# A decoder layer on one Trainium2 core: in the MLP's seven-product groups, two of the four weight sums are made by a GpSimd transfer that adds in SBUF, instead of by VectorE

## What is computed

```python
    merged = g[:, :, 0] * o_conv + g[:, :, 1] * o_fox + g[:, :, 2] * o_mem
    x = x + merged @ w_out
    h2 = _rms(x, norm2_g)
    x = x + jnp.square(jax.nn.relu(h2 @ w_up)) @ w_down
```

## Time and profile before

| | us |
|---|---|
| median of 3 runs (lowest, highest) | 1628.13 (1627.29, 1629.13) |
| the profiled execution | 1628.6 |
| its span in the profile | 1626.9 |
| busy: PE, DVE, ACT, POOL | 1616.9, 1169.6, 871.4, 4.8 |
| moved by DMA | 315.88 MB |

### The profile page before, as it was taken

One profiled execution on the slowest core, in us unless ns is written; L12 is line 12 of the kernel. 1 busy time (PEld: TensorE's weight loads), 2 busy tenths in 40 slices (PEclk: granted clock), 3 DMA queues, 4 the chain that ended last, 5 costly groups with the idle time before them and its releaser, 6 DMA issues.

```text
span 1626.9 us, 19902 instructions
## 1 busy us (share of the span) xinstructions
PE 1616.9 (99%) x7374; PEld 1339.8 (82%) x7374; DVE 1169.6 (72%) x1279; ACT 871.4 (54%) x1023; POOL 4.8 (0%) x13
## 2 busy tenths in 40 slices
PE   8999999999999999999999999999999999999998
PEld 7888888888888888888888888888888888888887
DVE  5856676555477777766765678887888788887777
ACT  5845445444455555544344566655665466556663
POOL 0000000000000000000000000000000000000000
PEclk9999999999999999999999999999999999999999
DMA  8856555555655666675565665566565655565554
GB/s 315 295 170 190 171 170 154 169 164 170 174 170 190 193 191 200 206 269 186 180 195 191 205 196 182 182 208 196 193 200 189 203 185 192 201 203 193 191 189 150
DMA packets 151780, 315.88 MB, mean 194 GB/s; under 512 B 9104, under 2 KB 9488, under 8 KB 150928
## 3 DMA queue, kind: packets, MB, share of 16 engines
q1 hardware_dynamic: 151696, 314.72, 61.0%
HBM read 312.59 MB, written 2.10 MB: 193 GB/s over the span
## 4 chain that ended last, share of the span: by engine, by line
PE 98%; DMA 1%; DVE 0%; ACT 0%; SPq 0%; issue 0%; DVEq 0%; ACTq 0%
PE bank L1954 42%; PE bank L1780 40%; PE bank L2057 9%; PE bank L1975 3%; PE bank L1799 2%; PE bank L1812 1%; DMA raw<-in_w_mem_kv 1%; PE bank L1907 0%; PE bank L1837 0%; PE bank L1868 0%; DVE wlo L1117 0%; PE bank L1927 0%; ACT whi L643 0%; PE bank L1832 0%; PE bank L1929 0%; DVE wide L1202 0%
## 5 line engine op out<-in xcount | busy, mean ns | idle before, releaser
L1117 DVE TENSOR_TENSOR wlo<-raw,whi 128x1024 fp32r<-128x1024 f32 x490 | 593.9, 1223 | 358.0 <-ACT whi L643 353.9
L643 ACT ACTIVATE whi<-raw 128x1024 fp32r<-128x1024 f32 x490 | 515.1, 1058 | 544.7 <-PE bank L1780 283.2
L1780 PE MATMUL bank<-whi,lhs_a 128*128 128x512 f32 x1280 | 400.5, 394 | 0.0
L1954 PE MATMUL bank<-whi,lhs_a 128*128 128x512 f32 x1248 | 385.0, 390 | 0.0
L1780 PEld LDWEIGHTS bank<-whi,lhs_a 128*128 128x128 f32 x1280 | 236.9, 188 | 46.8
L1954 PEld LDWEIGHTS bank<-whi,lhs_a 128*128 128x128 f32 x1248 | 233.7, 188 | 48.1
L1780 PE MATMUL bank<-wlo,lhs_a 128*128 128x512 f32 x640 | 249.8, 390 | 0.0
L1954 PE MATMUL bank<-wlo,lhs_a 128*128 128x512 f32 x624 | 242.9, 389 | 0.0
L1954 PE MATMUL bank<-whi,lhs_b 128*128 128x512 f32 x768 | 237.5, 390 | 0.0
L1954 PEld LDWEIGHTS bank<-whi,lhs_b 128*128 128x128 f32 x768 | 143.4, 188 | 29.4
L1780 PE MATMUL bank<-whi,lhs_b 128*128 128x512 f32 x512 | 158.1, 390 | 3.9 <-DVE wlo L1140 2.2
(11 more groups left out here) (241 smaller groups left out, 1503.5 us busy)
## 6 DMA issues: line engine op xcount, KB each, us to landing
raw<-in_w_in SPq DMA_DIRECT2D x208, 512.0 KB, 3.7
raw<-in_w_up SPq DMA_DIRECT2D x96, 512.0 KB, 4.0
raw<-in_w_down SPq DMA_DIRECT2D x96, 512.0 KB, 4.5
raw<-in_w_out SPq DMA_DIRECT2D x32, 512.0 KB, 3.7
raw_f<-in_w_up SPq DMA_DIRECT2D x16, 1024.0 KB, 5.0
raw_f<-in_w_down SPq DMA_DIRECT2D x16, 1024.0 KB, 5.0
raw<-in_w_mem_kv SPq DMA_DIRECT2D x30, 512.0 KB, 6.7
raw<-in_w_conv_out SPq DMA_DIRECT2D x16, 512.0 KB, 4.4
```

The source lines that it names most:

```text
L643: act.activation(whi[n % RING], raw[slot], ACT.Copy).then_inc(hi_ready, 1)
L1117: dve.tensor_tensor(wlo[n % RING], raw[plain(n) % RING], whi[n % RING].bitcast(F32), ALU.subtract).then_inc(lo_ready, 1)
L1780: last = pe.matmul(dst, lhs[:, part, k + kk, s], w[:, kk, :], start=(k + kk == 0 and i == 0), stop=(k + kk == tiles - 1 and i == 2))
L1954: last = pe.matmul(bank[2 * side + tok], lhs[:, part, PK * k + kk, P * tok:P * (tok + 1)], w[:, kk, :], start=(at + kk == 0 and i == 0), s ...
```

## The change

The weight sums are now made with plus signs, and the signs that this takes away move to the small sums of the activations (`s_sums`) and to the last step of `combine`. T1 and T3 are B11 + B12 and B22 + B12. They are made so:

- SP issues, ahead of each `raw_f` load, one more load of 512 KB that puts B12 twice (a repeated source) into `t_raw[:, 0:2]`. It waits for the same `lo_ready`, and also for `t_lo_ready` of the group before.
- GpSimd waits for this load (`t_begun`) and for `raw_f` (`fast_landed`), and issues a transfer from `raw_f[:, 1:3]` to `t_raw[:, 0:2]` in SBUF that adds. It signals `t_summed`.
- DVE's operation at line 1520 falls away. `t_sums` waits for `t_summed` and makes T2 and T4.
- ACT's first half of `t_hi` waits for `t_summed`, the second for T4.
- SP's loop over three quarters is written out.

```diff
             def load_ff(n, src):
                 if is_fast(n):
+                    q, blk, at, _ = ff_place(n)
                     if freed_by(n) < 0:
                         sp.wait_ge(merged_ready, NBD)
                     else:
-                        sp.wait_ge(lo_ready, base + (freed_by(n) + 1))
+                        sp.wait_ge(lo_ready, freed_by(n) + 1)
+                        sp.wait_ge(t_lo_ready, fast_index(q, blk, at))
+                    sp.dma_start(t_raw[:, 0:2, :], src[:, 0:1, 0:COLS].to_broadcast([P, 2, COLS])).then_inc(t_begun, 16)
                     sp.dma_start(raw_f[:].rearrange("p (k s) n -> p k (s n)", k=PK), src).then_inc(fast_landed, 16)
                     return
...
+            for f in range(FASTS * QUARTERS):
+                pool.wait_ge(t_begun, 16 * (f + 1))
+                pool.wait_ge(fast_landed, 16 * (f + 1))
+                pool.dma_start(t_raw[:, 0:2, :], raw_f[:, 1:3, :], accum_op=ALU.add).then_inc(t_summed, 16)
...
+                act.wait_ge(t_summed, base * 16 + 16 * (f + 1))
                 for h in range(2):
-                    act.wait_ge(t_made, base * 3 + (3 * f + 1 + 2 * h))
+                    if h:
+                        act.wait_ge(t_made, base * 2 + (2 * f + 2))
                     act.activation(t_hi[:, 2 * h:2 * h + 2, :], t_raw[:, 2 * h:2 * h + 2, :],
...
-                dve.tensor_tensor(s1, a21, a22, ALU.add).then_inc(s_made, 1)
+                dve.tensor_tensor(s1, a21, a22, ALU.subtract).then_inc(s_made, 1)
...
-                dve.tensor_tensor(s4, a12, s2, ALU.subtract).then_inc(s_made, 1)
+                dve.tensor_tensor(s4, a12, s2, ALU.add).then_inc(s_made, 1)
...
                 dve.wait_ge(fast_landed, base * 16 + 16 * (f + 1))
+                dve.wait_ge(t_summed, base * 16 + 16 * (f + 1))
                 b22, b21 = raw_f[:, 2, :], raw_f[:, 3, :]
-                dve.tensor_tensor(t_raw[:, 0:2, :], raw_f[:, 1:3, :], raw_f[:, 0:1, :].to_broadcast([P, 2, COLS]),
-                                  ALU.subtract).then_inc(t_made, 1)
-                dve.wait_ge(t_made, base * 3 + (3 * f + 1))
                 dve.tensor_tensor(t_raw[:, T_2, :], t_raw[:, T_1, :], b22, ALU.add).then_inc(t_made, 1)
-                dve.wait_ge(t_made, base * 3 + (3 * f + 2))
-                dve.tensor_tensor(t_raw[:, T_4, :], b21, t_raw[:, T_2, :], ALU.subtract).then_inc(t_made, 1)
+                dve.wait_ge(t_made, base * 2 + (2 * f + 1))
+                dve.tensor_tensor(t_raw[:, T_4, :], b21, t_raw[:, T_2, :], ALU.add).then_inc(t_made, 1)
...
-                    dve.tensor_tensor(comb[:, 0:2, :], comb[:, 2:5:2, :],
-                                      bank[P5].unsqueeze(1).to_broadcast([P, 2, COLS]),
-                                      ALU.subtract).then_inc(combined, 1)
+                    dve.tensor_tensor(comb[:, 0:2, :], bank[P5].unsqueeze(1).to_broadcast([P, 2, COLS]),
+                                      comb[:, 2:5:2, :], ALU.subtract).then_inc(combined, 1)
```

More of the change, by code:

```diff
@@ L432, in build @@
         fast_landed, fast_made = sem("fast_landed"), sem("fast_made")
+        t_begun, t_summed = sem("t_begun"), sem("t_summed")
         a_copied, s_made = sem("a_copied"), sem("s_made")
@@ L453, in build @@
         w_down = t["w_down"].rearrange("(q k p) n -> q p k n", p=P, k=KT)
-        w_down_rows = t["w_down"].rearrange("(k p) n -> p k n", p=P)
         def gate_half(jb, side):
@@ L563, in _, with load_ff @@
                         sp.dma_start(x_sb[:, tok, :], x_dram[:, tok, :]).then_inc(x_again[tok], 16)
-            def load_ff(n, src, base=0):
+            def load_ff(n, src):
                 if is_fast(n):
+                    q, blk, at, _ = ff_place(n)
                     if freed_by(n) < 0:
@@ L570, in load_ff @@
                     else:
-                        sp.wait_ge(lo_ready, base + (freed_by(n) + 1))
+                        sp.wait_ge(lo_ready, freed_by(n) + 1)
+                        sp.wait_ge(t_lo_ready, fast_index(q, blk, at))
+                    sp.dma_start(t_raw[:, 0:2, :], src[:, 0:1, 0:COLS].to_broadcast([P, 2, COLS])).then_inc(t_begun, 16)
                     sp.dma_start(raw_f[:].rearrange("p (k s) n -> p k (s n)", k=PK), src).then_inc(fast_landed, 16)
                     return
-                sp.wait_ge(lo_ready, base + (freed_by(n) + 1))
+                sp.wait_ge(lo_ready, freed_by(n) + 1)
                 slot = plain(n) % RING
                 sp.dma_start(raw[slot], src).then_inc(landed[slot], 16)
[L578 to L588, removed]
+            for q in range(QUARTERS):
+                for n in load_order(q):
                     _, blk, at, side = ff_place(n)
                     k = slice(PK * K_ORDER[blk][at], PK * (K_ORDER[blk][at] + 1))
-                    c = WIDE * (blk % UPS) + COLS * side
                     if is_fast(n) and side:
                         continue
+                    c = WIDE * (blk % UPS) + COLS * side
                     width = WIDE if is_fast(n) else COLS
[L595 to L599, removed]
+                    load_ff(n, w_up[:, k, D * q + c:D * q + c + width] if blk < UPS else
+                            w_down[q, :, k, c:c + width])
             for c in range(NBD - 1):
```

## The result

The changed kernel takes 1828.6 us (median of 4 runs, 1828.2 to 1832.2), against 1628.2 before: a ratio of 1.124, with a 95% interval of 1.122 to 1.126. It is 200 us slower. The forecast was 1781 with a range of 1690 to 1890: right in sign, in the mechanism of the wait and in the places, and 48 us short. The profiled execution took 1832.2 us, with a span of 1830.5.

The account below looks back on a forecast made before the run. TensorE alone was taken to bound the kernel in the MLP. To the profiled 1628.6 us the prediction added 120 of stalls and 33 of lower clock, 1781.6, so 1781 for the median; range 1690 to 1890.

Parts of the forecast that it names:

- type C: Second group of block 3, one a quarter: TensorE stalls 2.7 us, needing `fast_lower` for the second product.
- type A: Second group of blocks 0, 1, 2, three a quarter: TensorE stalls 2.7 us for group 6's left low part.
- type B: First group of blocks 1, 2, 3, three a quarter: TensorE stalls 6.4 us for group 1's left low part.
- The operations at line 1520, signs, list, the added wait for `t_lo_ready`: nothing: 39 us of DVE work goes, none on the chain; changed signs, written-out SP loop and added wait cost nothing.
- L = 5.6: Time from `raw_f` landing to `t_summed`, in all groups: 5.0 us transfer plus 0.6 to wake and issue; bounds 3.7 and 9.8.
- The additional load, 1.3 us: On SP's queue, 512 KB ahead of each `raw_f` delays its landing by 1.3 us; bounds 0 and 3.7.
- The clock, 12 falls of 2.7 us: TensorE's clock falls to 1.2 GHz at the 12 longest stalls (6.4 us), 2.7 us each, 33 us in all.
- The clock holds: Rival: TensorE's clock holds or rises at once after stalls, 1748 us; chance 0.2.
- Quick: Rival: adding transfer takes 3.7 us, like a plain load; kernel 1695 to 1728 us; chance 0.12.
- slow: Rival: adding transfer takes 8 to 9.8 us, perhaps sharing engines with weight loads; kernel 1891 to 1942 us; chance 0.17.
- Covered: Rival: transfer under 1.6 us leaves no stall, even at group 1's left low part; 1628 us; chance 0.02.
- DVE's relief pays: Rival: less DVE work helps where TensorE waits for DVE in the MLP; faster only by noise; chance 0.01.

Follow-up runs that it names:

- experiment 10: Transfer kept only in first groups of blocks 0, 1, 2, waits moved later in blocks 1, 2; DVE makes the other sums, against the changed kernel: 1630.0 us.
- experiment 1: Changed kernel without its transfers: DVE makes T1 and T3 again, with plus signs, and SP's loads stay written out: 1628.8 us.
- experiment 4: Changed kernel with the same transfers, but `t_sums` and `t_upper`, which wait for the sums, further down the lists of DVE and ACT: 1805.7 us.
- experiment 5: Changed kernel whose additional load reads two different tiles in place of one tile twice: 1787.2 us.
- experiment 2: Changed kernel without the adding transfer, DVE making T1 and T3; the additional load goes into a buffer nobody reads: 1686.7 us.
- experiment 6: Changed kernel without the additional load, except for the first group: 1762.8 us.
- experiment 7: Changed kernel with GpSimd's transfer as a plain copy in place of the add: 1788.4 us.
- experiment 9: Changed kernel with more TensorE work: 24 matmuls behind group 0 of blocks 1 to 3, 12 ahead of the other stalls: 1821.4 us.
- experiment 3: DVE makes T1 and T3; additional load and adding transfer go into an unread buffer, only the next `raw_f` load waits: 1687.6 us.

## Why the prediction was right, and where its sizes were off

*What bounds the kernel, and that relief of DVE is worth nothing.* Right, as far as experiment 10 shows it: there 15 us less on DVE bought nothing. What the 39 us did in the changed kernel can't be read by itself.

*The places.* Right: 28 stalls in three types and in the order forecast, none in the first group of block 0. At type C TensorE waits already before the first product, for `t_lo`, where I had it at the second, for `fast_lower`. Idle time was forecast at 12 x 6.4 + 12 x 2.7 + 4 x 2.7 = 120 us, and is 142. By type and weight, in the mean of one stall:

| type | forecast | `w_up` | `w_down` |
|---|---|---|---|
| A | 2.7 | 2.8 (8) | 4.8 (4) |
| B | 6.4 | 5.5 (4) | 6.8 (8) |
| C | 2.7 | | 6.0 (4) |

*The operations at line 1520, signs, list, the added wait for `t_lo_ready`: nothing.* Right for signs and list (experiment 1). For the added wait no run stands alone; in the trace of after SP issues the next load 0.02 us behind the end of `fast_lower` (1195.43 + 1.76, 1197.21).

*L = 5.6.* On the chain of the quarter shown it is 0.49 us of handing over and 4.7, 5.9, 5.4, 4.6, 4.6 and 4.5 us of transfer at types A and B, 5.4 together in the mean, and 5.3 over all 24. The nearest row (a load of 1 MB) was the right one, though by luck in part: a copy of 512 KB takes 3.4 us on this queue and the add 1.5 more. At type C it was 9.7, and 8.7 to 10.7 in the four quarters:

```profile
1346.62 0.49 issue
1347.11 9.19 DMA t_raw<-raw_f
```

This is the term that was mis-sized most at one place. My sum gave one L to all places, and type C is a place where the plain loads aren't held back: four of them, of `w_down`, are issued between 1341 and 1349 and land after a median of 6.7 us. That they are what slows the transfer is argued (experiment 4), not shown. The C interval grew by 8.4 us, where I had 1.3. Of the 7.1 between them 4.1 are L, 2.2 are `raw_f`, which was later than with `w_up`, and 0.7 the load, which left 1.0 us later behind the type B stall (6.1 against 5.1 us after TensorE's restart) and not 1.7. That is 28 us over four quarters.

*The additional load, 1.3 us.* Right for `w_up` (6.3), wrong for `w_down` (8.5, so 3.5), which at 16 stalls is 35 us more. The failed assumption is that a tile read twice costs what two tiles cost; experiment 5 shows 41 us for it.

*The clock, 12 falls of 2.7 us.* The mechanism was right, the count and the places were not. By the granted clock it fell at 26 of the 28 stalls. Behind 23 of them the first pair of matmuls already takes 1.0 to 1.2 us. Behind three of type A (2.9, 3.2 and 3.1 us of idle time, at 1247.64, 1470.09 and 1691.21) it takes 0.73 or 0.74, and the clock falls a little later, in the midst of work:

```profile
1244.00:1248.00 4.00, 1.11 (x6) 1.00 0.01 2
1248.00:1250.00 2.00, 2.00 (x8) 0.74 0.56 152
1250.00:1252.00 2.00, 2.00 (x6) 0.50 0.66 209
```

Only behind two stalls of 2.7 and 2.6 us (at 1025.11 and 1413.71) did it hold, while it fell at two of 2.4 and 2.5. So my division by type, falls at type B alone, was too neat. One type B stall, in stretches of 2 us (length, PE busy, granted clock, DMA share, GB/s):

```profile
1268.00:1270.00 2.00, 0.00 (x0) 0.86 0.00 0
1270.00:1272.00 2.00, 0.04 (x1) 0.50 0.00 0
1272.00:1274.00 2.00, 2.00 (x5) 0.50 0.43 120
1274.00:1276.00 2.00, 2.00 (x7) 0.50 0.63 220
1276.00:1278.00 2.00, 2.00 (x10) 0.93 0.54 173
```

The clock is at its lower level, 1.2 GHz, in the two stretches behind the restart and back in the third, which costs 1.0 + 1.0 + 0.1 = 2.1 us. In all, TensorE is busy for 62 / 26 = 2.4 us longer a fall. On the chain a fall costs 2.1 us here (18.4 - 16.3) and 2.2 in the mean of the eight type B stalls of blocks 1 and 2, and about as much at type C. It costs nothing at type A and at the type B stall of block 3, where TensorE isn't on the chain. That makes 12 places of 2.2, some 27 us. The term of 33 had the count of 12 by luck, with four of the twelve at the wrong place, and a price that was half a microsecond too high.

The Trainium skill ("TensorE: Matmul & The Clock Gate", section "Why this matters for your kernels") has the clock fall in idle gaps and rise with sustained work; this trace now shows both.

*The rivals.* "The clock holds" falls by the rows above. "Quick" and "slow" fall as rules for all groups; the slow one is true of type C alone. "Covered" and "DVE's relief pays" fall with the 28 stalls. Not one of my rivals was that the price depends on which weight is read.

*The 48 us that were missing.* The later `raw_f` of `w_down` gives 35, L at type C 4 x 4 = 16, the load behind type B 3, L at types A and B -7, and the clock -6: 41 of them.

By parts, the 200 us are: the additional load 58 (experiment 2) to 66 (experiment 6, where the transfer itself got slower), of which 41 by the repeated source; the rest, 134 to 142, the wait for the adding transfer, of which 40 is the adding (experiment 7). The clock's 27 are in these. The parts don't add up exactly, since the length of the transfer depends on what runs beside it.

## What to carry to other kernels

A transfer that takes work off an engine that isn't the bound is worth nothing, and where the buffer it reads is loaded just in time, its whole latency comes onto the chain; ask first how long the data lie there before somebody reads them, and put the transfer only where that is longer than the latency; even there it bought nothing here (experiment 10). In a list that is followed in order, what stands behind the wait pays, and moving the wait moves the bill unless each engine's list is looked at (experiment 4). A chain set by transfers doesn't get shorter by speeding up what lies beside it (experiment 9).

## What was not expected of the hardware

- A 512 KB load that reads one 256 KB tile twice lands after 3.8 us with rows 32 KB apart and after 6.3 with rows 8 KB apart, and the 1 MB load behind it lands after 6.3 and 8.5; two different tiles at the same place take 4.3 and 4.5.
- On GpSimd's queue, within SBUF: 512 KB copied 3.4 us, 512 KB added 4.9, 256 KB added 3.8, and 0.49 from the landing waited for to the issue. Beside other loads the add took 6.6 in the middle, and up to 10.2.
- 32 such transfers that DVE and ACT don't wait for changed the kernel's time by 1 us, within the noise (experiment 3).
- TensorE's granted clock fell at 26 of 28 stalls of 2.4 to 8.3 us, at three of them only after TensorE had gone on working.
